# Norm weights as rows on all partitions ahead of the transposes, and the last two chunks of two products by tile

## The reference, cut to what matters

```python
def rms_norm_2(x, g):
    xf = x.astype(jnp.float32)
    y = xf * lax.rsqrt(jnp.mean(xf * xf, axis=-1, keepdims=True) + EPS)
    return (y * g.astype(jnp.float32)).astype(x.dtype)

def hybrid_layer(x, mem, pos, layer_idx, norm_mix, norm_mem, w_in, w_mem_kv, w_out,
                 norm_ffn, w_gate_up, w_down):
    proj = rms_norm_2(x, norm_mix) @ w_in
    ...
    mo = memory_attention(qm, mem, norm_mem, w_mem_kv)   # begins with rms_norm_2(mem, norm_mem)
    x = x + jnp.concatenate([mix, mo], axis=-1) @ w_out
    x = x + swiglu_ffn(rms_norm_2(x, norm_ffn), w_gate_up, w_down)
    return x
```

## Time and profile before

| | us |
|---|---|
| median of 3 runs | 2604.73 (2604.55 to 2607.08) |
| the profiled execution, its own time | 2611.35 |
| its span, first to last instruction | 2609.6 |
| TensorE busy | 2341.2 |
| VectorE busy | 1514.2 |
| ScalarE busy | 988.6 |
| GpSimd busy | 187.9 |

### The profile page before, as it was taken

The page is one execution under the profiler, slowest core; times in us unless marked ns, Lnnn a source line. Parts: engine busy times, 40 slices in busy tenths (PEclk is TensorE's granted clock), DMA queues, the critical chain, the costliest instruction groups (busy, mean ns, idle before and its releaser), DMA issues. The chain is left out here.

```text
span 2609.6 us, 32919 instructions
## 1 busy us (share of the span) xinstructions
PE 2341.2 (90%) x12945; PEld 1944.3 (75%) x12945; DVE 1514.2 (58%) x2273; ACT 988.6 (38%) x1543; POOL 187.9 (7%) x235
## 2 busy tenths in 40 slices
PE   5888978999979999996898889899698899898998
PEld 2666746777757777786776679798597799697996
DVE  3499387645454444325964756665665565566564
ACT  4312265333233333223225544444343434344343
POOL 1053100100010000002420000000100000000000
PEclk7899989999979999997999999899896899899999
DMA  7222201443324444323321266465450366452664
GB/s 226 65 65 73 65 21 58 133 141 113 114 71 150 157 155 152 113 97 97 112 87 45 79 187 186 131 185 170 126 149 28 103 181 194 129 162 58 177 184 132
DMA packets 440188, 317.68 MB, mean 122 GB/s; under 512 B 25770, under 2 KB 379732, under 8 KB 440036
## 3 DMA queue, kind: packets, MB, share of 16 engines
q1 hardware_dynamic: 438500, 310.79, 39.8%
q0 software_dynamic: 1504, 4.79, 0.6%
q10 hardware_dynamic: 32, 0.01, 0.0%
HBM read 314.50 MB, written 1.05 MB: 121 GB/s over the span
## 5 line engine op out<-in xcount | busy, mean ns | idle before, releaser
L279 DVE TENSOR_TENSOR split<-raw,split 128x1024 fp32r<-128x1024 f32 (+1 forms) x602 | 717.6, 1203 | 754.7 <-ACT split L276 753.4
L290 PE MATMUL PS<-HH,split 128*128 128x256 f32 (+1 forms) x2504 | 820.5, 328 | 59.4 <-DVE HL L284 38.2
L276 ACT ACTIVATE split<-raw 128x1024 fp32r<-128x1024 f32 (+1 forms) x602 | 611.5, 1031 | 597.2 <-PE PS L292 476.3
L291 PE MATMUL PS<-HL,split 128*128 128x256 f32 (+1 forms) x2504 | 811.9, 324 | 0.0
L292 PE MATMUL PS<-HH,split 128*128 128x256 f32 (+1 forms) x2504 | 810.5, 324 | 0.0
L290 PEld LDWEIGHTS PS<-HH,split 128*128 128x128 f32 x2504 | 481.4, 192 | 114.4 <-DVE HL L284 41.4
L291 PEld LDWEIGHTS PS<-HL,split 128*128 128x128 f32 x2504 | 480.8, 192 | 39.2
L292 PEld LDWEIGHTS PS<-HH,split 128*128 128x128 f32 x2504 | 481.7, 192 | 37.9
L290 PE MATMUL PS<-split,UH 128*128 128x512 f32 x440 | 173.8, 395 | 0.0
L291 PE MATMUL PS<-split,UH 128*128 128x512 f32 x440 | 172.4, 392 | 0.0
L292 PE MATMUL PS<-split,UL 128*128 128x512 f32 x440 | 172.3, 392 | 0.0
(11 more groups left out here) (238 smaller groups left out, 2728.6 us busy)
## 6 DMA issues: line engine op xcount, KB each, us to landing
raw<-in_w_in_dram SPq DMA_DIRECT2D x120, 512.0 KB, 3.9
raw<-in_w_mod_dram SPq DMA_DIRECT2D x96, 512.0 KB, 4.5
raw<-in_w_ffn_in_dram SPq DMA_DIRECT2D x88, 512.0 KB, 3.9
raw<-in_l_w_gate_up_dram SPq DMA_DIRECT2D x88, 512.0 KB, 3.9
raw<-in_w_ffn_out_dram SPq DMA_DIRECT2D x44, 512.0 KB, 3.5
raw<-in_l_w_down_dram SPq DMA_DIRECT2D x44, 512.0 KB, 4.5
raw<-in_l_w_in_dram SPq DMA_DIRECT2D x30, 512.0 KB, 4.6
raw<-in_w_attn_out_dram SPq DMA_DIRECT2D x16, 512.0 KB, 4.7
```

The lines of the kernel that those rows point to most:

```text
L276: eng.activation(c["high"], c["raw"], ACT.Copy).then_inc(high_done, 1)
L279: eng.tensor_tensor(c["low"], c["raw"], c["high"].bitcast(F32), ALU.subtract).then_inc(low_done, 1)
L290: pe.matmul(out, a[0], b[0], start=first, stop=False)
L291: pe.matmul(out, a[0], b[1], start=False, stop=False)
```

## The change

It does four things.

1. In the second block the norm weights are loaded as rows on all 128 partitions (`GN` for n1, `FN` for n2 and then for the final norm), and DVE multiplies by rstd and the row in one SCALAR_TENSOR_TENSOR ahead of the transposes. ACT then copies each transposed bank to `HH` (rounding it), and DVE subtracts `HH` from the same bank into `HL`. The helpers are `norm2_act`, `norm2_dve` and `norm2_wait`.
2. POOL loads the rows: `GN` for E0 once all hidden tiles of the first block's last layer are written, `FN` with E0's tables, and after each n2 the next ones.
3. The six small loads of weight columns, their transpose and their copy are gone from the start.
4. `product` has an argument `last`; with 2, as in the second block's y and down products, the last two chunks of the second half are loaded together and multiplied tile by tile.

```diff
-    def product(T, pe, name, w, kts, cols, tiles, lhs, before=None):
+    def product(T, pe, name, w, kts, cols, tiles, lhs, before=None, last=1):
         width = min(512, cols)
         step = SLOT // width
-        for n in range(cols // width):
+        halves = cols // width
+        for n in range(halves):
             ps = {}
-            for k0 in range(0, kts, step):
-                i, ws = T.load(rows(w, k0, step, n * width, width), (step, width))
-                if k0 == 0:
+            starts = list(range(0, kts, step))
+            together = last if n == halves - 1 else 1
+            for c in range(0, len(starts) - together + 1):
+                mine = starts[c:] if c == len(starts) - together else starts[c:c + 1]
+                ws = [T.load(rows(w, k0, step, n * width, width), (step, width)) for k0 in mine]
+                if c == 0:
                     for t in tiles:
                         ps[t] = T.open((name, n, t))
-                for k in range(k0, k0 + step):
-                    if before and n == 0:
+                if len(mine) > 1:
+                    order = [(m, k, t) for t in tiles for m, k0 in enumerate(mine) for k in range(k0, k0 + step)]
+                else:
+                    order = [(0, k, t) for k in range(mine[0], mine[0] + step) for t in tiles]
+                for m, k, t in order:
+                    if before and n == 0 and t == tiles[0]:
                         before(k)
-                    for t in tiles:
-                        ins = multiply(pe, ps[t][:, 0:width], lhs(k, t), cut2(ws, slice(None), k - k0), k == 0, k == kts - 1)
-                        if k == kts - 1:
-                            T.close(ins, (name, n, t))
-                if k0 + step < kts:
+                    ins = multiply(pe, ps[t][:, 0:width], lhs(k, t), cut2(ws[m][1], slice(None), k - mine[m]), k == 0, k == kts - 1)
+                    if k == kts - 1:
+                        T.close(ins, (name, n, t))
+                if mine[-1] + step < kts:
                     T.mark(ins)
-                T.used(i)
+                for i, _ in ws:
+                    T.used(i)
...
+    def norm2_act(act, name, src, tiles, ready):
+        c = norm_cols(name)
+        def highs(n, t):
+            for g in range(2):
+                wait_result(act, (name, t, g))
+                to = (slice(None), slice(4 * g, 4 * g + 4), slice(t * P, (t + 1) * P))
+                act.activation(HH[to], bank((name, t, g)).rearrange("p (k c) -> p k c", k=4), ACT.Copy).then_inc(S(name + "_high"), 1)
+        for n, t in enumerate(tiles):
+            ready(act, t)
+            if n >= 2:
+                wait_result(act, (name, tiles[n - 2], 1))
+            act.activation(XN[:, n % 2, :], src(t), ACT.Square,
+                           accum_out=ss[:, c + n:c + n + 1]).then_inc(S(name + "_squares"), 1)
+            if n >= 1:
+                highs(n - 1, tiles[n - 1])
+        highs(len(tiles) - 1, tiles[-1])
+    def norm2_dve(dve, name, src, tiles, gain, ready):
+        c = norm_cols(name)
+        def lows(n, t):
+            for g in range(2):
+                dve.wait_ge(S(name + "_high"), 2 * n + g + 1)
+                to = (slice(None), slice(4 * g, 4 * g + 4), slice(t * P, (t + 1) * P))
+                read_out(dve.tensor_tensor(HL[to], bank((name, t, g)).rearrange("p (k c) -> p k c", k=4), HH[to].bitcast(F32),
+                                           ALU.subtract), (name, t, g))
+        for n, t in enumerate(tiles):
+            ready(dve, t)
+            dve.wait_ge(S(name + "_rstd"), n + 1)
+            dve.scalar_tensor_tensor(XN[:, n % 2, :], src(t), rstd[:, c + n:c + n + 1], gain(t), ALU.mult,
+                                     ALU.mult).then_inc(S(name + "_xn"), 1)
+            if n >= 1:
+                lows(n - 1, tiles[n - 1])
+        lows(len(tiles) - 1, tiles[-1])
+    def norm2_wait(pe, name, tiles):
+        for t in tiles:
+            for g in range(2):
+                wait_read(pe, (name, t, g))
...
+    GN = over((nc.sbuf_usable_end - 2 * D * 4) // 32 * 32, "GN", [P, 2, D])
...
-        for e in range(DEPTH):
-            for r, nm in enumerate(("norm_mix", "norm_mem", "norm_ffn")):
-                r0 = 24 * e + 8 * r
-                lst.append((stage_norms[r0:r0 + 8, :], A["l%d_%s_2" % (e, nm)].rearrange("(r p) -> r p", p=P)))
...
+    def mix_gains(pool, e):
+        for m, nm in enumerate(("norm_mix", "norm_mem")):
+            src = A["l%d_%s_2" % (e, nm)].rearrange("(o d) -> o d", o=1)
+            pool.dma_start(GN[:, m, :], src.broadcast_to([P, D])).then_inc(S("mix_gains"), 16)
...
+            if l == DEPTH - 1:
+                pool.wait_ge(S(L + "hidden"), FT)
+                mix_gains(pool, 0)
...
-            norm_wait(pe, L + "n1", [0, 1, 2, 3])
+            norm2_wait(pe, L + "n1", [0, 1, 2, 3])
...
-            product(T, pe, L + "y", pname(e, "w_out"), OUT_TILES[e], D, [0, 1], lefts((O2H, O2L)))
-            ffn_pe(T, pe, L, pname(e, "w_gate_up"), pname(e, "w_down"), [0, 1], SEQ, (UH2, UL2))
+            product(T, pe, L + "y", pname(e, "w_out"), OUT_TILES[e], D, [0, 1], lefts((O2H, O2L)), last=2)
+            ffn_pe(T, pe, L, pname(e, "w_gate_up"), pname(e, "w_down"), [0, 1], SEQ, (UH2, UL2), norm2_wait, last=2)
...
-            norm_act(act, L + "n1", lambda t: X[:, t, :], [0, 1, 2, 3], HF2, gain2(e, 0, 1), None, x2_ready(e, 0))
+            norm2_act(act, L + "n1", lambda t: X[:, t, :], [0, 1, 2, 3], x2_ready(e, 0))
...
+        def row_gain(nm, loaded):
+            pool.dma_start(FN[:, :], A[nm].rearrange("(o d) -> o d", o=1).broadcast_to([P, D])).then_inc(S(loaded), 16)
...
-                pool.dma_start(FN[:, :], A["final_norm_2"].rearrange("(o d) -> o d", o=1).broadcast_to([P, D])).then_inc(S("final_gain"), 16)
+                row_gain("l0_norm_ffn_2", "ffn_gain")
             rstd_pool(pool, L + "n2", [0, 1], D, "_rstd")
+            pool.wait_ge(S(L + "n2_xn"), 2)
+            if e == 0:
+                row_gain("l1_norm_ffn_2", "ffn_gain")
+                wait_result(pool, (L + "y", 1, 1))
+                mix_gains(pool, 1)
+            else:
+                row_gain("final_norm_2", "final_gain")
...
-            norm_dve(dve, L + "n1", lambda t: X[:, t, :], [0, 1, 2, 3], HF2, gain2(e, 0, 1), None, x2_ready(e, 0))
+            dve.wait_ge(S("mix_gains"), 32 * (e + 1))
+            norm2_dve(dve, L + "n1", lambda t: X[:, t, :], [0, 1, 2, 3], lambda t: GN[:, t // 2, :], x2_ready(e, 0))
...
-            norm_dve(dve, L + "n2", lambda t: X[:, t, :], [0, 1], HF2, gain2(e, 2), None, x2_ready(e, 1))
+            dve.wait_ge(S("ffn_gain"), 16 * (e + 1))
+            norm2_dve(dve, L + "n2", lambda t: X[:, t, :], [0, 1], lambda t: FN[:, :], x2_ready(e, 1))
```

More of the change, by code:

```diff
@@ L674, in build, with ffn_pe @@
     units_of = {l: [(t, h) for t in layer_tokens(l)[2] for h in range(HEADS)] for l in range(DEPTH)}
-    def ffn_pe(T, pe, L, w_up, w_down, tiles, n, U, fill=nothing, then=nothing):
+    def ffn_pe(T, pe, L, w_up, w_down, tiles, n, U, wait, fill=nothing, then=nothing, last=1):
         norm_pe(T, pe, L + "n2", tiles)
-        norm_wait(pe, L + "n2", tiles)
+        wait(pe, L + "n2", tiles)
         for j in range(FT):
@@ L685, in ffn_pe @@
         then()
-        product(T, pe, L + "ffn", w_down, FT, D, tiles, lefts(U), before=lambda k: pe.wait_ge(S(L + "hidden"), k + 1))
+        product(T, pe, L + "ffn", w_down, FT, D, tiles, lefts(U), before=lambda k: pe.wait_ge(S(L + "hidden"), k + 1), last=last)
     def ffn_act(act, L, n, tmp, fill=nothing):
@@ L1576, in x2_ready @@
         return wait
-    def gain2(e, which, mem_which=None):
-        def col(k, t):
-            c = 24 * e + 8 * (mem_which if mem_which is not None and t >= 2 else which) + k
-            return cols2[:, c:c + 1]
-        return col
     @block2.scalar
```

12 lines of the change are left out of this document (4 added, 8 removed).

## The result

The changed kernel took 2589.56 us (median of four runs, 2584.80 to 2591.97) against 2605.90 us for the kernel before in the same comparison (2604.55 to 2612.01). The profiled executions show it too: span 2585.8 us against 2609.6.

What follows compares the result with a forecast made beforehand. TensorE, busy 90% of the span, plus its standstills at the norms was taken as the bound. Terms -0.8 + 7.0 - 3.6 - 4.5 - 3.6 - 1.2 = -6.7 us took the median from 2604.73 to 2598.0, range 2591.5 to 2605.0.

Steps and rivals of the forecast that it cites:

- E0 n2, -3.6: Second norm of layer E0: TensorE restarts earlier after the last product matmul, gaining 3.6 us, range 2.5 to 5.5.
- E1 n2, -3.6: Second norm of layer E1: same code and times as E0's second norm, so again 3.6 us gained.
- E1 n1, -4.5: First norm of layer E1, four tiles: TensorE restarts at 2273.6, not 2278.05, gaining 4.5 us, range 3 to 6.
- The end, -1.2: Final norm: tile 0 ready early, so Y of tile 1 starts sooner, gaining 1.2 us (0.8 to 1.4).
- E0 n1, +7.0: First norm of layer E0: weight splits slip behind the rope angles, delaying the third chunk; 7.0 us lost, range 5 to 8.2.
- a loss of 5.6: E0's first norm: alternative loss if harmless PSUM subtractions let GpSimd's table loads land earlier; 5.6 us rather than 7.0.
- The start, -0.8: Program start: six small loads and one transpose go while weight chunks are waited for, gaining 0.8 us (0 to 2).
- The copies and subtractions: In the norms: ScalarE copies out of PSUM at 0.60 us each, VectorE subtractions at 0.69 us each.
- the slower rival: Norms: PSUM subtraction into the fp32r tile is dear; at 1.6 us each, 2612.6 us in total; chance 4%.
- Row weights eating gains: Rival: row weights collide with down weights (4 us), or tables land at 1879.5; total about -2, 2602.7 us; chance 15%.
- The clock holds: Rival: TensorE's clock holds in the two shorter norm stalls, about 2.4 us more per site, 2593.2 us; chance 12%.
- The rival at 2587 us: E0's first norm: splits don't move or TensorE doesn't wait; 4 us gained there, total -18; chance 3%.

Runs made afterwards that it cites:

- before_moved: Kernel before with only `cols2` moved to the end of SBUF, so the rings and tiles behind start 192 bytes earlier: 2598.74 us, ratio 0.9962.
- by_chunk: Changed kernel without the order by tile (both calls lose `last=2`): its span ended 9.1 us later than the changed kernel's.
- keep_2: Changed kernel with the splits of coming weight chunks put back into the norm's loop on VectorE: span 3.9 us shorter than the changed kernel's.
- pad_192: Changed kernel with 192 unused bytes where `cols2` lay, restoring the old tile places: median 2608.1 us, 0.9986 of the kernel before.
- split_4_again: Repeat of the changed kernel with splits back in the norm's loop and four chunks split ahead of the angles: 2579.05 us, ratio 0.9873 to the kernel before.
- pad_64: Changed kernel with 64 unused bytes where `cols2` lay: span 2598.6 us.
- pad_160: Changed kernel with 160 unused bytes where `cols2` lay: span 2595.9 us.
- split_moved: Kernel before with 64 unused bytes between the raw slots and the split slots: 6.8 us off the span.
- best: split_4 with 32 unused bytes ahead of the first block's rings alone: 2570.81 us, ratio 0.9847 to the kernel before.
- again_after: The changed kernel once more, no edit, on another chip and in another run: 2588.03 us, ratio 0.9913.
- pad_32: Changed kernel with 32 unused bytes where `cols2` lay: 2590.31 us, ratio 0.9900.
- split_4: As keep_2, with the third and fourth chunks too split ahead of the angles on ScalarE and VectorE: 2571.06 us in a single look.

## Why the prediction was wrong

**The sum was made of the right parts, and the time was still wrong.** By its own steps, against the measured:

- *E0 n2, -3.6*: restart after 8.48 us instead of 11.48, -3.0. The forecast had 7.5 to 8.1; what it left out is the 0.4 us between the end of the last subtraction (2058.66) and the matmul. *E1 n2, -3.6*: 8.04 for 11.45, -3.4.
- *E1 n1, -4.5*: 14.35 for 19.09, -4.7; in the column before_moved it is 4.4.
- *The end, -1.2*: -1.3, and by_chunk shows that the order by tile is what pays there. The same order keeps GpSimd's ms clear of XN in the norms, at 1.1 to 1.7 us a restart, which the text had as "hidden" without a price of its own.
- *What a restart is worth.* The sum counted each gain at the restart as a gain of the program. In the next full stretch of matmuls the three are 2.8, 3.8 and 1.7 us against the kernel before, and 3.6, 4.4 and 2.7 against before_moved; a restart that comes earlier can meet more of the low clock, as the two windows under by_chunk show.
- *E0 n1, +7.0*: the mechanism was right and keep_2 shows it. Up to the attention the changed kernel lost 6.2 us against the kernel before and 6.9 against before_moved. It came in parts, though. The third chunk lost 5.1 and not 7.0, since the angles started 19.1 us behind the first square where 20.9 had been allowed for: GpSimd issued the large tables 13.6 us behind it, not 15.2. It did so because the fourth square came 9.6 us behind the first, not 11.3; ScalarE no longer waited for VectorE to free `HF2`. From issue to landing the tables took 4.1 to 4.9 us, before 4.0 to 5.6. The prediction's estimate that drew on the Trainium skill (SBUF — State Buffer, Who interferes with whom), a loss of 5.6, came nearer than 7.0, but the trace doesn't show that a shared port was the reason. Some 0.3 us arose ahead of the first square, and the other 0.8 to 1.5 between the third chunk and the attention, which the sum had at nothing. Behind the third chunk the changed kernel had the clock low for 10.2 us, the kernel before for 6.8.
- *The start, -0.8*: not measurable. At the 150th matmul the changed kernel is 0.9 us ahead of the kernel before and 1.7 behind before_moved, and traces with the changed kernel's first block differ by 1.6 there.
- *The copies and subtractions*: 0.60 and 0.69 us, as the rows of other operations had promised; the slower rival is out. *Row weights eating gains*: out as well; the loads behind E0 n2 do not show in any restart. *The clock holds*: no; it was low in the transposes of tile 1 in E0 n2 (1.97 us for eight).

Together, in full stretches and with the end, that is 9.6 us gained and 6.2 lost against the kernel before, 12.0 and 6.9 against before_moved, where the terms without the start had 12.9 and 7.0: 3 to 5 us for 5.9. The 7.0 us between the spans of the changed kernel and before_moved are near the 6.7 of the sum partly by luck: before_moved was 2.0 us ahead up to E0 and lost 4.1 to the clock in E0's attention. (The bounds of the terms add to -15.4 and -0.6, where the text has about -14 and 0; the range does not hang on it.)

**The step that failed** stands in no term. It is that the sum ended there: "At the start, six small loads [...] and one transpose go" took the loads and the transpose into account and not the 192 bytes in which they ended, and everything without a term of its own was carried over as unchanged. The removed tile moved an operand of every product with split weights. That missing term measures 16.3 us between the steps of the two traces; pad_192, which puts the places back, has 16.5 in the steps, 14.3 between the spans and 20 between the medians, and before_moved gains 11 by median. About 1.7 of the 23.8 between the two spans are clock, by their length at this place: the kernel before had 3.4 us at the low clock at the start of the first block's last down product, where the same code after had none. by_chunk and split_4_again, which have the changed kernel's first block, had it too, so it belongs to the execution. Before, where that product starts at 1789:

```profile
1790.00:1800.00 10.00, 10.00 (x36) 7.24 (x36) 2.98 (x3) 4.26 (x5) 0.00 (x0) 0.85 0.23 78
```

After, where it starts at 1779:

```profile
1780.00:1790.00 10.00, 10.00 (x45) 8.07 (x44) 3.72 (x4) 5.06 (x6) 0.00 (x0) 1.00 0.61 211
```

The rival at 2587 us would have had the number and not the reason: the splits did move, and TensorE did wait.

What stays open: by which rule the place acts, which of the tiles beside the split slots takes part, what picks the step anew from layer to layer, and why the first block gives 342 in before_moved and by_chunk and 345 in the changed kernel with the same places.

## What to carry to other kernels

When a change adds or drops a tile, compare where the tiles behind it lie before putting the rest down as unchanged, and look at the number of matmuls in a full stretch of code that nobody touched. To time such a change fairly, pad the hole, or free it in both kernels, and do both, since here the two gave 2 and 11 us. Then try a few pads on purpose, for each ring by the width of the matmuls that it feeds. And when a helper is written anew, look for what the old one did on the side: a split that slips behind a long block on an in-order engine costs the whole block.

## What the runs showed of the hardware

**The place in SBUF changes TensorE's step at full clock.** 116.7 to 120.0 ns for 256 columns, 227.6 or 232.8 to 233.5 for 512, with no wait, the clock at 1.00 and the instructions alike. Not every product feels it: the first block's down products (`UH` and `UL` against split weights, 512 columns) stepped at 226.7 to 226.8 ns in all fourteen traces, though their operands moved as well. Nobody would see it in the mean length of a matmul, which overlaps its neighbours: 0.28 us in both kernels.

**The clock came back at different moments in the same code.** In E0's attention the changed kernel had its clock back among the last groups:

```profile
2013.00:2016.00 3.00, 3.00 (x15) 2.88 (x15) 0.17 (x2) 1.39 (x3) 0.00 (x0) 0.50 0.00 0
2016.00:2019.00 3.00, 3.00 (x26) 3.00 (x25) 2.10 (x7) 1.87 (x4) 0.00 (x0) 0.86 0.01 3
```

keep_2 was 7.1 us ahead there, ran the same instructions, and got it back 10.7 us later, counted from the same matmul of the attention:

```profile
2012.00:2015.00 3.00, 3.00 (x17) 3.00 (x16) 0.46 (x2) 0.97 (x2) 0.00 (x0) 0.50 0.00 0
2015.00:2018.00 3.00, 3.00 (x16) 3.00 (x16) 0.59 (x3) 0.23 (x1) 0.00 (x0) 0.50 0.00 0
```

It costs 4.1 us, the step from -7.1 to -3.0 in the table. before_moved, by_chunk and pad_64 show the same step, pad_160, split_moved and best one of 5.1 to 5.3 us, again_after, pad_192, pad_32 and split_4 none, and split_4's repeat has it again. What makes it was not tried.
